# One GpSimd operation instead of two for each level of the triangular inverse, in the RWKV stage of a two-model transformer kernel

## What is computed

```python
def step(state, inp):
    r_t, w_t, k_t, v_t, a_t, b_t = inp
    sa = jnp.einsum('bhvk,bhk->bhv', state, a_t)
    state = (state * w_t[:, :, None, :] + sa[..., None] * b_t[:, :, None, :]
             + v_t[..., None] * k_t[:, :, None, :])
    return state, jnp.einsum('bhvk,bhk->bhv', state, r_t)
```

## Time and profile before

| | before |
|---|---|
| median of three runs | 3940.07 us |
| span of the profiled execution | 3931.4 us |
| TensorE matmul busy | 3743.9 us, 95% |
| VectorE busy | 1848.1 us, 47% |
| ScalarE busy | 1581.7 us, 40% |
| GpSimd busy | 1779.5 us, 45% |
| the 192 mask operations | 157.4 us busy, 843 ns each |

### The profile page before, as it was taken

How to read it: one execution, slowest core, us unless ns; L and a number is a source line. 1 busy time by engine, 2 the same in 40 slices (tenths; PEclk the granted TensorE clock), 3 DMA queues, 4 the chain that set the end, 5 groups by cost and what they waited for, 6 DMA issues and landing times. The chain is left out here.

```text
span 3931.4 us, 72626 instructions
## 1 busy us (share of the span) xinstructions
PE 3743.9 (95%) x30890; PEld 3040.7 (77%) x30904; DVE 1848.1 (47%) x2868; ACT 1581.7 (40%) x2643; POOL 1779.5 (45%) x1132
## 2 busy tenths in 40 slices
PE   7999989999998999998999999899999999999998
PEld 6777758878887777776887887677878877787887
DVE  7777652155635877754226553543231133423112
ACT  5555352343334555535234333454332234433222
POOL 5555444434445555544443444463444435344443
PEclk9999999989998999999998999899999999999999
DMA  4111203335532211122334553212222221222322
GB/s 142 52 56 56 88 28 135 99 134 193 183 107 76 92 51 56 56 99 72 99 105 143 189 182 104 69 65 76 97 86 97 97 85 66 70 96 87 97 97 86
DMA packets 108753, 379.88 MB, mean 97 GB/s; under 512 B 12560, under 2 KB 12944, under 8 KB 107792
## 3 DMA queue, kind: packets, MB, share of 16 engines
q1 hardware_dynamic: 102816, 365.66, 27.8%
q10 hardware_dynamic: 5616, 9.58, 0.7%
HBM read 359.46 MB, written 15.73 MB: 95 GB/s over the span
## 5 line engine op out<-in xcount | busy, mean ns | idle before, releaser
L299 POOL TENSOR_TENSOR Wlo<-raw,Whi 128x1024 fp32r<-128x1024 f32 (+1 forms) x744 | 1385.8, 1876 | 1671.6 <-ACT Whi L284 1671.4
L232 PE MATMUL ps<-hh,Whi 128*128 128x512 f32 x2864 | 1150.9, 402 | 22.1 <-DVE hl L383 10.1
L232 PE MATMUL ps<-hl,Whi 128*128 128x512 f32 x2864 | 1125.3, 393 | 0.0
L232 PE MATMUL ps<-hh,Wlo 128*128 128x512 f32 x2864 | 1124.4, 393 | 0.1
L284 ACT ACTIVATE Whi<-raw 128x1024 fp32r<-128x1024 f32 x552 | 578.7, 1054 | 689.3 <-PE ps L232 617.8
L232 PEld LDWEIGHTS ps<-hh,Whi 128*128 128x128 f32 x2864 | 543.3, 190 | 147.8 <-issue 15.7
L232 PEld LDWEIGHTS ps<-hh,Wlo 128*128 128x128 f32 x2864 | 543.0, 190 | 116.2 <-issue 0.5
L232 PEld LDWEIGHTS ps<-hl,Whi 128*128 128x128 f32 x2864 | 543.8, 190 | 108.1 <-issue 1.9
L232 PE MATMUL ps<-gh,Whi 128*128 128x512 f32 x864 | 337.9, 391 | 3.8 <-POOL Wlo L299 3.8
L232 PE MATMUL ps<-gh,Wlo 128*128 128x512 f32 x864 | 336.5, 390 | 0.0
L232 PE MATMUL ps<-gl,Whi 128*128 128x512 f32 x864 | 336.5, 389 | 0.0
(11 more groups left out here) (365 smaller groups left out, 5652.8 us busy)
## 6 DMA issues: line engine op xcount, KB each, us to landing
raw<-in_stream SPq DMA_DIRECT2D x554, 512.0 KB, 3.3
ada<-in_ada SPq DMA_DIRECT2D x96, 512.0 KB, 4.3
park_x<-xT SPq DMA_DIRECT2D x2, 2048.0 KB, 7.3
park_yh<-yh ACTq DMA_DIRECT2D x16, 256.0 KB, 2.1
park_yl<-yl ACTq DMA_DIRECT2D x16, 256.0 KB, 2.5
xT<-park_x SPq DMA_DIRECT2D x2, 2048.0 KB, 8.3
yrh<-park_yh SPq DMA_DIRECT2D x16, 256.0 KB, 5.1
yrl<-park_yl SPq DMA_DIRECT2D x16, 256.0 KB, 4.9
```

The source lines that it names most:

```text
L232: last = pe.matmul(ps, left[a](k), right[c](k), start=start and k == 0 and i == 0, stop=stop and k == n - 1 and i == 2)
L299: last = pool.tensor_tensor(b["Wlo"][:, slot, part], b["raw"][:, raw_slot(b, u), part], b["Whi"][:, slot, part].bitcast(F32), SUB)
```

## The change

From level 1 on, one GpSimd operation masks both heads (128x512) where there were two of 128x256. For that, `TM` is laid out by level slot first and head second, so that the two heads of a slot are adjacent. Level 0 keeps one operation for each head. The merged mask of level 2 waits for T01, and a higher one for TensorE's reading of head 1 of level l-2; the numbers of the semaphore steps (`INV_G`) follow. TensorE, VectorE and ScalarE do what they did, at the new addresses.

```diff
-INV_G = Steps("m00", "m01", *[f"m{l}{h}" for l in range(1, LEVELS) for h in range(2)])
+INV_G = Steps("m00", "m01", *[f"m{l}" for l in range(1, LEVELS)])
...
-            pe.wait_ge(s["inv_g"], INV_G(p, f"m{l}{h}"))
+            pe.wait_ge(s["inv_g"], INV_G(p, f"m{l}"))
...
-                    last = into(u, 2 + h, c, b["TM"][half(1 - u), h, l % 2], b["X"][half(1 - u), h])
+                    last = into(u, 2 + h, c, b["TM"][half(1 - u), l % 2, h], b["X"][half(1 - u), h])
...
-    for l in range(LEVELS):
-        for h in range(2):
-            if l == 0:
-                pool.wait_ge(s["inv_a"], INV_A(p, f"d{h}1"))
-            else:
-                if l >= 2:
-                    pool.wait_ge(*((s["inv_p"], INV_P(p, f"W{l - 2}{h}")) if l > 2 else (s["inv_v"], INV_V(p, f"T0{h}"))))
-            pool.tensor_tensor(blocks(b["TM"][:, h, l % 2]), blocks(b["TD"][:, h]), lvl[:, l].broadcast_to([P, BLK, CB]), MUL)                 .then_inc(s["inv_g"], 1)
+    for h in range(2):
+        pool.wait_ge(s["inv_a"], INV_A(p, f"d{h}1"))
+        pool.tensor_tensor(blocks(b["TM"][:, 0, h]), blocks(b["TD"][:, h]), lvl[:, 0].broadcast_to([P, BLK, CB]), MUL).then_inc(s["inv_g"], 1)
+    between(0)
+    for l in range(1, LEVELS):
+        if l == 2:
+            pool.wait_ge(s["inv_v"], INV_V(p, "T01"))
+        elif l > 2:
+            pool.wait_ge(s["inv_p"], INV_P(p, f"W{l - 2}1"))
+        pool.tensor_tensor(blocks(b["TM"][:, l % 2].rearrange("j h n -> j (h n)")), blocks(b["TD"][:].rearrange("j h n -> j (h n)")),
+                           lvl[:, l].broadcast_to([P, 2 * BLK, CB]), MUL).then_inc(s["inv_g"], 1)
         between(l)
```

More of the change, by code:

```diff
@@ L941, in rwkv_diagonal_act @@
         if p:
-            act.wait_ge(s["inv_g"], INV_G(p - 1, f"m{LEVELS - 1}{h}"))
+            act.wait_ge(s["inv_g"], INV_G(p - 1, f"m{LEVELS - 1}"))
         for u in range(2):
@@ L1153, in rwkv_inv_dve @@
         dve.wait_ge(s["inv_g"], INV_G(p, f"m0{h}"))
-        dve.tensor_tensor(blocks(b["Wc"][:, h]), blocks(b["TM"][:, h, 0]), ident, ADD).then_inc(s["inv_v"], 1)
+        dve.tensor_tensor(blocks(b["Wc"][:, h]), blocks(b["TM"][:, 0, h]), ident, ADD).then_inc(s["inv_v"], 1)
         dve.wait_ge(s["inv_v"], INV_V(p, f"i{h}"))
@@ L1158, in rwkv_inv_dve @@
         for u in range(2):
-            dve.tensor_tensor(blocks(b["XT"][half(u), h]), blocks(b["TM"][half(1 - u), h, 0]), ident[half(1 - u)], ADD) \
+            dve.tensor_tensor(blocks(b["XT"][half(u), h]), blocks(b["TM"][half(1 - u), 0, h]), ident[half(1 - u)], ADD) \
                 .then_inc(s["inv_v"], 1)
```

## The result

The changed kernel takes 3969.88 us (median of four runs, 3969.33 to 3971.23), the one before 3940.35 in the runs beside it: a ratio of 1.0081, interval 1.0069 to 1.0093. It is slower, by 29.5 us. The forecast was 3971.

The account below looks back on a forecast made before the run. TensorE, 95% busy, was taken to wait on VectorE's chain, lengthened by GpSimd operations. Longer stalls (19 us) plus clock drops (12 us) gave 31 us: span 3962, run time 3971 us, range 3943 to 3984; slower 0.79.

Parts of the forecast that it names:

- VectorE's chain sets the stall: VectorE's chain before level 2 grows 1.36 us a turn, TensorE's stall from 2.26 to 3.6; 14 turns, 19 us.
- the first addition: First L1154 on VectorE, beside merged m1: ends at 227.94 instead of 227.40, +0.54 us.
- the first XT fill: First L1159 on VectorE moves behind r1, which then has the port: +0.19 us.
- The scans: VectorE's scans: first runs free, -0.45 us; second and third meet merged m2 and m3, +1.08 us.
- dz to kkr: Last scan, dz, k and kkr on VectorE meet k1 to k4 instead of m30, m31, k1, k2: 0.
- The first turns: The two first turns, which also wait for VectorE, grow like the 12 with the stall: 1.36 us each.
- The merged operation: GpSimd's 512-wide mask takes 1.28 us like bt, not kh's 1.04; GpSimd saves 16 us, all beside the path.
- The clock: TensorE's granted clock drops to 1.2 GHz after more stalls: seven more, up to 1.7 us each, 12 us.
- The conversion to the runs' time: Median of runs lies 8.7 us above the profiled span: span 3962 us becomes 3971 us.
- A fixed cost of a meeting: Same-time rival: VectorE waits a fixed 0.4 us whatever GpSimd's width; time 3940 us, chance 0.12 including masks missing the chain.
- a repeated mask leaves the port free: Faster rival: VectorE operations beside merged m1, m2, m3 run at own length, saving 21 us: 3919 us, chance 0.09.

Follow-up runs that it names:

- the first experiment: Changed kernel with two 256-wide masks a level again, its layout of TM and later waits kept: 3938.19 us beside 3938.25, ratio 0.9999.
- the second's: Changed kernel with only levels 4 and 5 merged, layout kept: 3938.16 us, ratio 0.9996 to the kernel before.
- changed kernel with filler: Changed kernel plus nine matmuls with overwritten results in each turn with a stall before level 2: 3953.80 us, ratio 1.0041 to the kernel before.
- pieces of 512: Kernel before, masks untouched, units r and k split in two pieces of 128x512 instead of four of 128x256: 3968.95 us, ratio 1.0082.
- pieces of 128: Kernel before, masks untouched, units r and k split in eight pieces of 128x128 instead of four of 128x256: 3900.98 us, ratio 0.9914.

## Why the prediction was right, and where it was off

**VectorE's chain sets the stall.** Right. +1.36 us a turn was forecast, +1.44 measured, and the stall is 3.7 us for 3.6. By its steps: the first addition +0.56 for +0.54, of which the second gives back 0.10, since it no longer meets a mask (0.38 for 0.48); the first XT fill meets r1, and the four fills take 0.32 us more for 0.19; the scans +0.70 for +0.63, the first at its own length and two beside merged masks; dz to kkr unchanged, since k3 and k4 reached the chain. The first turns grew by 1.5 us, so that 14 turns are 20 us, where 19 stood. One reading behind it was wrong, without effect on the sum. I took 0.48 us for the own length of L1154, but the one of that length (227.81) had itself met m11, which runs to 228.01; without a mask it takes 0.38. So VectorE goes on 0.1 us before GpSimd's operation ends, not 0.2, in the kernel before and after alike.

**The merged operation.** Right: 1.30 us alone, as for bt (1.28) and not for kh (1.04). In the chain the 80 of them average 1375 ns:

```profile
L1148 POOL TENSOR_TENSOR TM<-TD,const 128x512 f32<-128x512 f32 x80 | 109.4, 1375 | 137.8 <-PE ps L719 131.2 <-DVE XT L1162 6.6
```

With the 23.8 us of the single ones that is 133 us, where it was 157: GpSimd won 24 us, forecast at 16, and nothing of it came back. m4 and m5, the later waits and the addresses cost nothing that the times show, as the first two experiments tell.

**The clock.** The term was in the sum, and its size came out right in part by luck: both its factors were off, in opposite directions. I took three drops in four stalls, seven more than before; every one of the 14 turns had one, 11 more. And I took 1.7 us for each. What one costs can be read from the distance between two starts of level 2: two turns of the kernel before, without and with a drop, then a turn of the changed kernel with one, and of the changed kernel with filler without (length, busy us of the matmuls, granted clock, DMA share and GB/s).

```profile
288.51:336.73 48.22, 45.94 (x992) 1.00 0.18 57
336.73:386.52 49.79, 47.48 (x992) 0.97 0.16 55
```

```profile
200.15:251.16 51.01, 47.27 (x993) 0.97 0.16 54
```

```profile
297.63:347.33 49.70, 47.98 (x1001) 1.00 0.17 56
```

A drop costs 1.6 us in the kernel before and 1.3 in the changed one. 11 drops at 1.3 are 14 us, where 12 was forecast, an estimate from these rows. With the 20.6 us of the stalls that makes 35 of the 36.2 us by which the span grew.

**The conversion to the runs' time** was wrong, and hidden by luck. I put 8.7 us between span and run. The changed kernel's profiled run took 3969.45 us with a span of 3967.6, so only 1.9 lie around it, and the other runs have 1.8 or 1.9 too. The 3931.4 of before must then have been a run near 3933, at the low end of its spread (3930 to 3942 in all chips' runs). The span forecast, 3962, was 5.6 us too short and the conversion 6.8 too long; in 3971 the two cancel.

By spans the change is 36.2 us, not the 31 of the sum; by medians 29.5. The likely difference is how often the kernel before drops its clock: behind three stalls in its profiled run, but behind five in the first experiment's and seven in the second's, two kernels of equal time. The drops of its other runs aren't on record.

**The rivals.** A fixed cost of a meeting would have given 3925 with pieces of 512 and 3938 with pieces of 128; 3969 and 3901 were measured. That a repeated mask leaves the port free is refuted by the scans beside it, 1.44 us each where they need 0.39. The page of the Trainium skill that names two SBUF inputs as in contention (GPSIMD Engine Reference, Specifications) agrees with these scans, and with fills of 0.85 us beside 256-wide operations where 0.42 is their shortest; the rule in Advanced Engine Details and Errata, VectorE Performance Modes, names two-port modes only and would have left scans and fills untouched.

## What to carry to other kernels

Where VectorE is on the path and its operations read two SBUF operands, a GpSimd operation beside it is paid for by its length. (A second tile isn't always needed: kkr multiplies one tile by a column, and it takes 0.83 to 0.85 us beside the pieces of k and 0.49 alone. The transposes, also of one tile, keep their 0.45 us beside m11.) Fewer and longer GpSimd operations save GpSimd's own time and lengthen VectorE's. Look for VectorE operations with a median far above their shortest, see which GpSimd operations run beside them, and split those or move them to where VectorE reads PSUM or waits. And count a longer stall of TensorE with what the granted clock does behind it.

## What was not expected of the hardware

Halving the width of GpSimd's pieces, with twice as many operations, was worth 35 us (3936.4 to 3901.0). Longer stalls are followed by the lower clock level much more often than in proportion: none of 12 at 1.7 us in the kernel with filler, three of 12 at 2.3 us in the kernel before and five of 12 in the first experiment, nine of 12 at 3.0 us with level 1 merged, 12 of 12 at 3.7 us in the changed kernel. Its two first turns, with stalls of 2.2 and right after it 1.2 us, had one too. And nine idle-time matmuls a turn made a kernel 16 us faster.
